# A mixture-of-experts block whose weight ring is fourteen slots long in the expert stage, in place of eight

## What is computed

```python
def ec_moe(h, w_router, w_gate_e, w_up_e, w_down_e):
    cap = EC_CAPACITY * l // N_EXPERTS                    # 64 tokens for each of 16 experts
    aff = jax.nn.softmax((h @ w_router).astype(jnp.float32), axis=-1)
    top_aff, top_idx = lax.top_k(jnp.swapaxes(aff, 1, 2), cap)
    def per_set(hs, idx, wgt):
        xs = hs[idx]
        a = jax.nn.silu(jnp.einsum('ecd,edf->ecf', xs, w_gate_e)) * jnp.einsum('ecd,edf->ecf', xs, w_up_e)
        y = jnp.einsum('ecf,efd->ecd', a, w_down_e) * wgt[..., None].astype(hs.dtype)
        return jnp.zeros_like(hs).at[idx.reshape(-1)].add(y.reshape(-1, hs.shape[-1]))
```

## Time and profile before

| | us |
|---|---|
| median of 3 runs | 3795.51 |
| lowest and highest | 3790.4, 3802.41 |
| the profiled execution, its own time | 3791.34 |
| its span from the first to the last instruction | 3789.5 |

### The profile page before, as it was taken

How to read it: one execution, slowest core, us unless ns; L and a number is a source line. 1 busy time by engine, 2 the same in 40 slices (tenths; PEclk the granted TensorE clock), 3 DMA queues, 4 the chain that set the end, 5 groups by cost and what they waited for, 6 DMA issues and landing times.

```text
span 3789.5 us, 29989 instructions
## 1 busy us (share of the span) xinstructions
PE 3562.0 (94%) x12000; PEld 1683.5 (44%) x12000; DVE 907.4 (24%) x1750; ACT 643.4 (17%) x1328; POOL 154.6 (4%) x114
## 2 busy tenths in 40 slices
PE   7999986999997998999999999999989999999998
PEld 2464433333232446545455444444554454544443
DVE  1341113211114415425112000032281431310000
ACT  1112010000002314314112000022160240210000
POOL 3300000000001000000000000000000000000000
PEclk9968997999998998999999999999889999999999
DMA  5013424999994121121221222212202212222211
GB/s 215 28 40 131 158 75 166 360 367 355 363 361 181 51 78 62 35 71 45 77 90 62 77 78 69 78 61 73 83 24 67 72 45 78 78 73 78 78 67 56
DMA packets 119226, 436.16 MB, mean 115 GB/s; under 512 B 13232, under 2 KB 13488, under 8 KB 118448
## 3 DMA queue, kind: packets, MB, share of 16 engines
q1 hardware_dynamic: 116208, 423.15, 30.6%
q10 hardware_dynamic: 2880, 11.09, 0.8%
HBM read 432.09 MB, written 2.10 MB: 115 GB/s over the span
## 4 chain that ended last, share of the span: by engine, by line
PE 80%; DMA 8%; DVE 7%; ACT 3%; DVEq 1%; issue 1%; POOL 0%; ACTq 0%; SPq 0%
PE bank L495 78%; DMA ring<-in_stream 8%; PE bank L836 2%; DVE arena L1629 1%; DVE arena L1654 1%; DVE arena L1651 1%; DVEq L1628 0%; DVE h L1258 0%; DVE bank L1620 0%; ACT arena L1112 0%; POOL sq L1241 0%; DVE arena L1258 0%; DVE arena L1253 0%; DVE arena L1378 0%; DVE arena L1336 0%
## 5 line engine op out<-in xcount | busy, mean ns | idle before, releaser
L495 PE MATMUL bank<-h,ring 128*128 128x512 f32 x3152 | 1370.7, 594 | 14.2 <-DVE h L1265 6.9
L495 PEld LDWEIGHTS bank<-h,ring 128*128 128x128 f32 x3152 | 598.2, 190 | 769.5 <-issue 757.9
L495 PE MATMUL bank<-arena,ring 128*128 128x512 f32 (+2 forms) x1936 | 750.8, 544 | 22.4 <-DVE arena L1581 10.7
L495 PEld LDWEIGHTS bank<-arena,ring 128*128 128x128 f32 x1936 | 365.3, 203 | 398.9 <-issue 367.7
L495 PE MATMUL bank<-ring,arena 128*64 128x512 f32 (+2 forms) x1856 | 463.1, 611 | 61.4 <-DMA ring<-in_stream 46.8
L495 PE MATMUL bank<-arena 128*64 128x128 f32 (+9 forms) x3016 | 457.9, 356 | 27.7 <-ACT arena L1102 8.4
L495 PEld LDWEIGHTS bank<-arena 128*64 128x64 f32 (+2 forms) x3016 | 289.0, 185 | 158.4 <-issue 85.8
L495 PEld LDWEIGHTS bank<-ring,arena 128*64 128x64 f32 (+2 forms) x1856 | 122.1, 137 | 390.2 <-DMA ring<-in_stream 216.7
L495 PE MATMUL bank<-y,ring 128*128 128x512 f32 x608 | 265.9, 597 | 11.9 <-DVE arena L1581 7.3
L1041 ACT ACTIVATE sig<-bank 128x512 f32<-128x512 f32 x106 | 63.4, 598 | 1123.1 <-PE bank L495 1123.1
L1241 POOL TENSOR_TENSOR sq<-sq 128x512 f32<-128x512 f32 (+1 forms) x68 | 80.4, 1183 | 3470.1 <-ACT sq L977 3470.1
(11 more groups left out here) (191 smaller groups left out, 1426.3 us busy)
## 6 DMA issues: line engine op xcount, KB each, us to landing
ring<-in_stream SPq DMA_DIRECT2D x807, 512.0 KB, 5.5
x<-in_xT ACTq DMA_DIRECT2D x1, 2048.0 KB, 11.1
arena<-in_memT ACTq DMA_DIRECT2D x2, 1024.0 KB, 4.8
outT<-h ACTq DMA_DIRECT2D x8, 256.0 KB, 2.6
arena<-in_ctxT ACTq DMA_DIRECT2D x1, 1024.0 KB, 16.0
y<-in_inv ACTq DMA_DIRECT2D x1, 1024.0 KB, 21.0
arena<-in_pr ACTq DMA_DIRECT2D x1, 636.5 KB, 5.4
arena<-in_cse ACTq DMA_DIRECT2D x1, 544.5 KB, 4.8
```

The source lines that it names most:

```text
L495: ins = pe.matmul(out, lhsT, rhs, start=start, stop=stop, skip_group_check=loose)
```

## The change

In the expert stage six more slots of 512 KB, at the end of `arena` (columns 21968 to 28112), are part of the ring. `ring_places` works out for each slot its place, the slot that had the place before (`BEFORE`), and how many times that place has been filled (`LANDINGS`). The 384 expert slots go round 14 places: first the eight of `ring` in their old order, then the six new ones. The first six slots that go into `arena` have no slot before them; for them SyncE's queue waits for the first of the eight products `out`. The layers go round the eight old places, in the order in which the last experts' slots leave them: their first two slots follow the expert slots 370 and 371, their next six follow 378 to 383. There are 14 semaphores `landed` in place of 8. The matmuls, their order, the number and size of transfers and their order in the queue stay as they are.

```diff
--- before.py
+++ after.py
@@ -50,6 +50,26 @@
 
 SLOTS_ONE, SLOTS_EXPERT, SLOTS_LAYER = slots_of(TILES_ONE), TILES_EXPERT // SLOT, slots_of(TILES_LAYER)
 SLOTS = SLOTS_ONE + E * SLOTS_EXPERT + LAYERS * SLOTS_LAYER
+MORE = 6
+
+
+def ring_places():
+
+    first = [(SLOTS_ONE + i) % RING for i in range(RING)]
+    wide = first + list(range(RING, RING + MORE))
+    place = [s % RING for s in range(SLOTS_ONE)] + [wide[e % (RING + MORE)] for e in range(E * SLOTS_EXPERT)]
+    order = [p for p in place[-(RING + MORE):] if p < RING]
+    place += [order[i % RING] for i in range(LAYERS * SLOTS_LAYER)]
+    last, before, count, used = {}, [], [], {}
+    for s, p in enumerate(place):
+        before.append(last.get(p))
+        last[p] = s
+        used[p] = used.get(p, 0) + 1
+        count.append(used[p])
+    return place, before, count
+
+
+PLACE, BEFORE, LANDINGS = ring_places()
 
 
 def numbered(stages):
@@ -246,6 +266,12 @@
         top8 = carve(8)[0:E, :]
 
 
+        more = arena[:, ARENA - MORE * SLOT * P:ARENA].rearrange("p (s c) -> p s c", s=MORE)
+        assert where[0] <= ARENA - MORE * SLOT * P
+
+        def slot_tile(p):
+            return ring[:, p, :] if p < RING else more[:, p - RING, :]
+
         where[0] = 0
         cosT, sinT, cosM, sinM = [carve(T) for _ in range(4)]
         pr2 = carve(N_PR2)
@@ -294,7 +320,7 @@
             return cse[:, o:o + w]
 
 
-        landed = [sem(f"landed{i}") for i in range(RING)]
+        landed = [sem(f"landed{i}") for i in range(RING + MORE)]
         slot_read = sem("slot_read")
         loaded = sem("loaded")
         loaded_pr1 = sem("loaded_pr1")
@@ -451,9 +477,11 @@
                     sp.wait_ge((gate_made, up_made, gate_made, up_made, y_made, y_made)[step],
                                2 * pair + (0, 0, 1, 1, 0, 1)[step] + 1)
             for s in range(SLOTS):
-                if s >= RING:
-                    wait_free(s - RING)
-                sp.dma_start(ring[:, s % RING, :], stream[s]).then_inc(landed[s % RING], 16)
+                if BEFORE[s] is not None:
+                    wait_free(BEFORE[s])
+                elif s >= RING:
+                    sp.wait_ge(made1, ONE["out"] + 1)
+                sp.dma_start(slot_tile(PLACE[s]), stream[s]).then_inc(landed[PLACE[s]], 16)
 
 
         @block.tensor
@@ -470,9 +498,9 @@
                     s = self.pos // SLOT
                     assert (self.pos + n - 1) // SLOT == s
                     if s == self.seen:
-                        pe.wait_ge(landed[s % RING], 16 * (s // RING + 1))
+                        pe.wait_ge(landed[PLACE[s]], 16 * LANDINGS[s])
                         self.seen += 1
-                    a = ring[:, s % RING, (self.pos % SLOT) * P:(self.pos % SLOT + n) * P]
+                    a = slot_tile(PLACE[s])[:, (self.pos % SLOT) * P:(self.pos % SLOT + n) * P]
                     self.pos += n
                     return a
```

## The result

| | before | after |
|---|---|---|
| median | 3796.9 us (3790.4 to 3802.41, 4 runs) | 3732.07 us (3729.38 to 3739.54, 4 runs) |
| ratio, 95% interval | | 0.9833 (0.9812 to 0.9854) |
| the profiled execution, its span | 3791.34, 3789.5 us | 3729.38, 3727.6 us |
| expert stage in the profile | 543.6 us | 482.9 us |

The forecast was 3730.2 us, in a range of 3720 to 3752. In what follows L523, L1102, L828 and L484 are the lines of the changed kernel that were L495, L1074, L800 and L456 before.

What follows compares the result with a forecast made beforehand. TensorE bounds the kernel, but ring transfers bound its expert stage: 1.1 + 3.3 + 472.3 + 0.6 + 1.0 = 478.3 us against 543.6, 65.3 less. Median 3795.51 - 65.3 = 3730.2 us, range 3720 to 3752.

Steps and rivals of the forecast that it cites:

- The stage is the place, and gaps in the transfers the cause: Expert stage: transfers stop during TensorE's rests at gather and spread, losing 8.2 us of a 69.5 us pair.
- the rivals of the rate: Expert stage: 363 GB/s is all memory gives, about 3791 us (0.05); or rate falls to 344 GB/s, 3820 us (0.05).
- The sum: Expert stage: 478.3 us against 543.6, so 65.3 us less.
- The start: Stage begin: first refill issued after 1.1 us, landing 3.3 us later, plus 0.6 us for the slower rate.
- The pace: Expert stage: after the first refill the other 369 slots follow at 1.28 us each, 472.3 us.
- A pair of 61.4 us: Expert stage: without gaps a pair takes 48 slots x 1.28 = 61.4 us, where it took 69.5.
- The count by landings: Spread and gather: fourteen slots leave no gap, with 5.9 and 4.6 us to spare; ten and eleven would do.
- The head start: Before the expert stage: six extra slots land by about 590.1, 33 us before first use; uncovered they cost 7.7 us.
- TensorE as the bound: Rival, expert stage: two more microseconds of waits make a pair 63.5 us, 50 us saved, 3745 us; chance 0.12.
- What costs nothing: Semaphores, addresses, extra waits and transfers into arena add nothing; the layers' 2622 us should not move.

Runs made afterwards that it cites:

- a line of four: Changed kernel with fourteen slots, each expert-stage slot issued only once the transfer four before it has landed; 3756.65 us, one run.
- the eleven: Changed kernel with three extra slots in place of six, eleven in all; 3750.48 us, ratio 0.988 against the kernel before.
- the twelve: Changed kernel with four extra slots in place of six, twelve in all; 3739.53 us, ratio 0.9859 against the kernel before.
- the stage without it: Changed kernel, but the six arena slots load only once the first expert slot has been read; 3737.46 us, ratio 0.9844, stage 490.2 us.
- alone: Changed kernel, but the six extra slots are loaded ahead and used once, then the eight old places serve; 3790.44 us, ratio 0.9987.
- half the bytes: Changed kernel, each expert slot after the first fourteen loaded only in its first half (256 KB), TensorE's work the same; 3716.0 us, one run.
- nineteen slots: Changed kernel with five more slots, three in y and two in h, all eleven extra loadable before the stage; 3720.53 us, ratio 0.9807.

## Why the prediction was right

**The stage is the place, and gaps in the transfers the cause.** Right. The stage lost 60.7 us, its neighbours are unchanged, and 410 GB/s held for the whole stage: over 459 us, from 644 on, the windows read

```profile
644.00:1103.00 459.00, 445.34 (x2080) 175.32 (x2076) 83.38 (x120) 26.84 (x48) 0.00 (x0) 1.00 1.03 409
```

That settles the rivals of the rate. Neither is a mean of 363 GB/s all that the memory gives over time, nor does the rate fall when TensorE is dense. The limit of some 358 GB/s from the Trainium skill ("DMA: Bandwidth & Descriptors", Specifications), by which a pair would have taken 70.3 us, isn't what one core on its own meets here.

**The sum.** 65.3 us forecast for the stage, 60.7 in the profile, 64.8 between the medians. That the median came within 1.9 us of the forecast is in part luck: the stage fell 4.6 us short of it, and differences between executions made up for it. The stage's 478.3 us were 4.6 too few, in two terms.

The start: the slot with which TensorE is first starved, the 29th, is read at 645.92, 24.8 us into the stage; by the prediction's terms it is 1.1 + 3.3 + 14 x 1.28 + 0.6 = 22.9. The first refill landed at 625.60, 4.5 us into the stage, where 4.4 had been worked out. The two behind it took 1.3 us more than their 1.28 each, in the window in which the rate is low although TensorE reads at full pace:

```profile
623.00:629.00 6.00, 6.00 (x32) 2.00 (x30) 0.00 (x0) 0.60 (x1) 0.00 (x0) 1.00 0.92 319
```

A single late landing, at 640.76, cost 1.1 us more. 0.6 us had been allowed for all this. So TensorE came to the first gather starved, where the prediction had one slot in hand.

The pace: from 645.92 to the last slot at 1103.04, 355 slots took 457.1 us, 1.288 us each and not 1.28, which is 2.7 us. It isn't a slower pace all along: the landings stand 1.28 us apart, but two of them, at 857.15 and 1090.19, come 2.80 and 2.78 us after the one ahead. Ahead of each of these two and of the one at 640.76, by 2.3 to 2.7 us, an instruction load of 16 KB begins, like those in the run with a line of four. The other loads of the stage show no late landing here, so the coincidence isn't an explanation.

**A pair of 61.4 us.** Right for four of six (61.38 to 61.40, the spacing of down products). The first took 62.65: it began with nothing in hand and ended with one slot landed and unread, 49 landings in all, and what is in hand isn't lost. The fourth took 62.95 and holds the late landing of 857.15. From one starved read to the same read of the next pair it is 61.39 us before it, 62.95 over it and 61.40 after it:

```profile
813.45 1.08 PE L523 MATMUL bank<-ring,arena 128*64 128x512 f32 x4 [0.17 <-DMA ring<-in_stream]
...
876.40 10.78 PE L523 MATMUL bank<-arena 128*64 128x512 f32 x28 [0.20 <-DMA arena<-in_stream]
...
937.80 1.08 PE L523 MATMUL bank<-ring,arena 128*64 128x512 f32 x4 [0.20 <-DMA ring<-in_stream]
```

The rate reads 409 GB/s all the same. It is what all 16 DMA engines move together, while TensorE waits for all 16 increments of a slot's semaphore, so a single part that is late would be enough; that this is what happened is not shown.

**The count by landings.** Right in its use, that fourteen leave no gap, and wrong in the sentence that ten slots would do at the spread and eleven at the gather. At the spread the margin was 5.9 us, as predicted: the first refill after it lands 9.2 us after its issue, where 3.3 would do. At the gather it took the line as full, and it isn't: between the two rests TensorE isn't starved, and one slot stands landed. The refill issued at 970.71 lands 6.7 us later, so the margin is 3.4 us and not 4.6. With the same 1.2 us off, eleven slots fall 0.5 us short at the gather and twelve have 0.8 to spare, and so it was: the refill of the eleven issued at 920.83 landed 1.82 us after the slot ahead of it, that of the twelve 1.49. What the count left out altogether is that the rate sags at the end of the line, with two or three transfers under way, before it is empty; twelve still lost 1.8 us at the gather looked at.

**The head start.** 7.7 us forecast, 7.3 in the stage without it, 5.4 by the medians; alone it is worth 1.2 us by the profile's stage (542.4, from a single profile) and 4.1 by the medians (against 3794.5 in its group), with an interval from 0.03% to 0.23% of the time, which is 1 to 9 us; pairs of 70.1 us ate part of it. Head start and depth add up within that scatter.

**TensorE as the bound.** Its own time was worked out as 60.1 to 61.5 us and is 60.5. The rival would have needed two more microseconds of waits a pair; with half the bytes they would have shown, and they don't.

**What costs nothing.** Transfers into `arena` beside its readers: 409 GB/s, no loss. The layers: 2623.6 us against 2622.4, and 2629.0 with nineteen slots, so that is what executions differ by.

## What to carry to other kernels

A mean rate under the engines' rate need not be a bandwidth bound: look at short windows, and if the full rate stands in the starved ones, what is missing is depth. The depth needed is what lands during the longest stretch in which the consumer reads nothing, plus what it has in hand when that begins, plus the lag of a refill; work it out for each rest in its order and not from a full line. Here it is 9.1 us of gather, 7.1 slots, one in hand, and 1.1 + 3.3 us of lag, 3.4 slots: 11.5, and twelve indeed left no gap in the landings. Add a slot or two, since just closing the gap leaves a slow stretch about it (62.9 us a pair with twelve, 61.9 with fourteen). With transfers and the engine within 2% of each other, further depth still gained here, by letting the engine run ahead over the first half of the stage, and SBUF that other stages have left is where it was to be had.

## What was unexpected of the hardware

After a gap, or with few transfers in line, the rate is low for 5 to 6 us although TensorE asks for more than the engines can give: 319 GB/s from 623 to 629 with a share of 0.92. From 629 to 640 it is 414 with TensorE as dense as before, so the reader's density isn't the cause. Why the first transfers after a gap are slow, the traces don't show.

A late landing may come of one packet of instructions, and with a short line it costs more; the traces show it as a coincidence only: with four transfers under way all 17 loads of 16 KB in the expert stage have a late landing behind them (and behind the one at 906.4 the rate is 309 GB/s from 912 to 918); with up to 13 under way it is 3 of 17.

SyncE's queue takes in only so many transfers. The issues into `y` with nineteen slots (duration in ns, minimum, median, maximum; then the time to landing):

```profile
L496 SPq DMA_DIRECT2D y<-in_stream x51: 327/1077/2982, 662.0 to 1046.8; - x51
...
DMA to landing us min/median/max: 10.6/15.3/16.7
```

An issue takes 0.33 us as a rule; for these the median is 1.08 us, and the landing lies at most 16.7 us behind the issue, which is 13 transfers of 1.28 us. Counting issues and landings one by one, no more than 13 slots are ever under way, with nineteen slots as with fourteen, and with fourteen the issue that makes it 12 takes 1.03 us in the median, those below it 0.33. So 12 or 13 of this size are under way and the next issue waits. It costs nothing here, since the engines are fed all the same, but a slot beyond that is stock and not line.
